# A fourth joined product in the first MLP stage, with high and low parts of the operands side by side

## What is computed

```python
def _squared_relu_mlp(h, w1, w2):
    return jnp.square(jax.nn.relu(h @ w1)) @ w2

def reference(x, norm_mix_g, norm_ffn_g, even_w_in, even_b_f, even_w_out,
              odd_w_in, odd_w_out, ffn_w_in, ffn_w_out, final_g):
    for layer in range(DEPTH):                                   # DEPTH = 2
        h = _rms_norm(x, norm_mix_g[layer])
        ...
        h = _rms_norm(x, norm_ffn_g[layer])
        x = x + _squared_relu_mlp(h, ffn_w_in[layer], ffn_w_out[layer])
    return _rms_norm(x, final_g)
```

## Time and profile before

| | |
|---|---|
| median of 3 runs | 1250.47 us (1250.42 to 1250.6) |
| the profiled execution | 1250.86 us, span of its instructions 1249.1 us |
| TensorE matmul busy | 1238.4 us, 99% |
| VectorE busy | 955.2 us, 76% |
| ScalarE busy | 768.6 us, 62% |
| GpSimd busy | 297.0 us, 24% |
| granted TensorE clock, mean | 0.998 |
| DMA moved | 238.93 MB, 191 GB/s |

### The profile page before, as it was taken

The page is one execution under the profiler, slowest core; times in us unless marked ns, Lnnn a source line. Parts: engine busy times, 40 slices in busy tenths (PEclk is TensorE's granted clock), DMA queues, the critical chain, the costliest instruction groups (busy, mean ns, idle before and its releaser), DMA issues.

```text
span 1249.1 us, 18840 instructions
## 1 busy us (share of the span) xinstructions
PE 1238.4 (99%) x7158; PEld 1080.3 (86%) x7158; DVE 955.2 (76%) x1232; ACT 768.6 (62%) x1064; POOL 297.0 (24%) x330
## 2 busy tenths in 40 slices
PE   9999999999999999999999999999999999999997
PEld 6788888898898988989898889898889889898896
DVE  6588647599779697798666797567898967869678
ACT  6688755477564575665656645456667647456474
POOL 2343653111211112101231212231221122111220
PEclk9999999999999999999999999999999999999999
DMA  7367567788988989974968588879589899898992
GB/s 246 97 137 163 136 148 191 205 210 190 225 223 219 233 189 211 225 218 114 224 135 199 131 227 180 210 155 234 101 222 243 207 203 226 217 232 202 210 215 99
DMA packets 147978, 238.93 MB, mean 191 GB/s; under 512 B 51104, under 2 KB 72872, under 8 KB 147888
## 3 DMA queue, kind: packets, MB, share of 16 engines
q0 software_dynamic: 32352, 102.79, 43.8%
q1 hardware_dynamic: 115232, 134.60, 34.1%
q10 hardware_dynamic: 304, 0.33, 0.1%
HBM read 127.57 MB, written 2.11 MB: 104 GB/s over the span
## 4 chain that ended last, share of the span: by engine, by line
PE 91%; DVE 3%; DMA 2%; issue 1%; ACT 1%; POOL 0%; SPq 0%; POOLq 0%; DVEq 0%; ACTq 0%
PE banks L1042 21%; PE banks L1420 12%; PE banks L1010 11%; PE banks L1211 7%; PE banks L969 6%; PE banks L1488 6%; PE banks L1002 5%; PE banks L1370 5%; PE banks L1151 4%; PE banks L1005 2%; PE banks L1434 2%; PE banks L1312 2%; PE banks L1178 2%; PE banks L1384 1%; DMA raw_tiles<-raw_tiles 1%
## 5 line engine op out<-in xcount | busy, mean ns | idle before, releaser
L2294 DVE TENSOR_TENSOR w<-raw_tiles,w 128x1024 fp32r<-128x1024 f32 x312 | 371.1, 1220 | 55.7 <-ACT w L1630 55.4
L1630 ACT ACTIVATE w<-raw_tiles 128x1024 fp32r<-128x1024 f32 x312 | 315.2, 1051 | 123.7 <-PE banks L1042 61.9
L1042 PE MATMUL banks<-w,arena_q 128*128 128x512 f32 x1332 | 304.3, 390 | 0.0
L3283 POOL DMA_DIRECT2D raw_tiles<-raw_tiles x176 | 152.3, 907 | 629.1 <-DVE w L2294 378.6
L1042 PEld LDWEIGHTS banks<-w,arena_q 128*128 128x128 f32 x1332 | 249.3, 188 | 51.7 <-DVE x L2620 0.4
L1420 PE MATMUL banks<-w,h_ops 128*128 128x512 f32 x672 | 154.2, 390 | 0.0
L1420 PEld LDWEIGHTS banks<-w,h_ops 128*128 128x128 f32 x672 | 125.6, 188 | 25.7
L1010 PE MATMUL banks<-h_ops,w 128*128 128x256 f32 x1152 | 140.1, 283 | 0.0
L1010 PEld LDWEIGHTS banks<-h_ops,w 128*128 128x128 f32 x1152 | 139.4, 192 | 0.7
L1002 PE MATMUL banks<-h_ops,w 128*128 128x512 f32 x288 | 102.3, 400 | 0.1
L969 PE MATMUL banks<-h_ops,w 128*128 128x256 f32 x672 | 82.0, 284 | 0.0
(11 more groups left out here) (247 smaller groups left out, 1864.9 us busy)
## 6 DMA issues: line engine op xcount, KB each, us to landing
raw_tiles<-raw_tiles POOLq DMA_DIRECT2D x176, 512.0 KB, 5.6
raw_tiles<-in_ffn_w_in SPq DMA_DIRECT2D x64, 512.0 KB, 6.3
raw_tiles<-in_ffn_w_out SPq DMA_DIRECT2D x64, 512.0 KB, 6.4
raw_tiles<-in_odd_w_in SPq DMA_DIRECT2D x32, 512.0 KB, 5.5
raw_tiles<-in_even_w_in SPq DMA_DIRECT2D x48, 256.0 KB, 3.4
raw_tiles<-in_odd_w_in SPq DMA_DIRECT2D x32, 256.0 KB, 5.0
raw_tiles<-in_odd_w_out SPq DMA_DIRECT2D x16, 512.0 KB, 6.3
raw_tiles<-raw_tiles POOLq DMA_DIRECT2D x20, 256.0 KB, 4.1
```

Source lines behind the costliest of these rows:

```text
L1042: mm = pe.matmul(bank[first + t][:, :], a_ring[a_slot(g, i)][:, a, k, P * t:P * t + P], w_slots[use_slot(use)][:, b, k, :], start=(starts ...
L1630: nc.scalar.activation(w_flat(use_slot(use), 0, half), raws[tile][:, 1024 * half:1024 * half + 1024], ACT.Copy).then_inc(m_hi, 1)
L2294: nc.vector.tensor_tensor(w_flat(use_slot(use), 1, half), raws[use_tile(key)][:, 1024 * half:1024 * half + 1024], w_flat(use_slot(use), 0, ...
L3283: pool.dma_start(raws[dst][:, part], raws[src][:, part], accum_op=ALU.add).then_inc(t_made[value][half], 16)
```

## The change

The operands' buffer becomes [block, k, 512 columns] with the low part's 256 columns directly behind the high part's, so that a joined matmul reads one run of 512. Product 7 of the first stage of wide groups becomes joined too. Its high-by-low half is in the upper half of the banks, so that ScalarE now copies (two `last_copy`), VectorE adds (two `wide_last`), and ScalarE makes one relu over the whole block in place of two from the bank. ScalarE makes both copies between the two weight halves. On VectorE the weight halves of the second stage's operand 2 move ahead of the sum S2, around the two adds. Groups 0 and 4 keep their order.

```diff
-WIDE = (1, 2, 3)
+WIDE = (1, 2, 3, 6)
...
-        h_ops = nc.alloc_sbuf_tensor_at("h_ops", [P, 8, 2, 4, 256], F32R, offset=h_at)
+        h_wide = nc.alloc_sbuf_tensor_at("h_wide", [P, 8, 4, 512], F32R, offset=h_at)
+        h_ops = h_wide[:, :, :, :].rearrange("p e k (a n) -> p e a k n", a=2)
...
-                                pe.matmul(dst.rearrange("p (q n) -> p q n", q=2), w_slots[use_slot(use)][:, 0, k, c:c + P],
-                                          h_ops[:, H_BLOCK[op], :, k, :],
+                                pe.matmul(dst, w_slots[use_slot(use)][:, 0, k, c:c + P], h_wide[:, H_BLOCK[op], k, :],
                                           start=(i < 3 and k == 0), stop=(k == 3), skip_group_check=True)
...
             def relu_last(g, b):
 
                 act.wait_ge(p_done, use_done(first_use(g, 6), b))
-                if g % CHUNKS == 0:
-                    act.wait_ge(hs_lo, 8 * (g // CHUNKS) + 4)
-                src = wide_part(6, b, LOW) if g % CHUNKS else pair_of(FIRST_X, b)
-                nc.scalar.activation(hidden_part(0, b, HIGH), src, ACT.Relu).then_inc(last_relu, 1)
+                act.wait_ge(hs_lo, 8 * (g // CHUNKS) + 4)
+                nc.scalar.activation(hidden_part(0, b, HIGH), pair_of(FIRST_X, b), ACT.Relu).then_inc(last_relu, 1)
+
+            def last_copy(g, b):
+
+                act.wait_ge(p_done, use_done(first_use(g, 6), b))
+                act.wait_ge(a_lo, 7 * g)
+                nc.scalar.activation(hidden_part(0, b, HIGH), wide_part(6, b, LOW), ACT.Copy).then_inc(last_copied, 1)
+
+            def wide_relu_last(g):
+
+                act.wait_ge(last_sum, wide_count(g) + 2)
+                block = a_blocks(1)["12"]
+                nc.scalar.activation(block, block, ACT.Relu).then_inc(last_relu, 2)
...
-                w_hi(stage + 1, 1, 0)
-                relu_last(g, 0)
-                w_hi(stage + 1, 1, 1)
-                relu_last(g, 1)
+                if g % CHUNKS:
+                    w_hi(stage + 1, 1, 0)
+                    last_copy(g, 0)
+                    last_copy(g, 1)
+                    w_hi(stage + 1, 1, 1)
+                    wide_relu_last(g)
+                else:
+                    w_hi(stage + 1, 1, 0)
+                    relu_last(g, 0)
+                    w_hi(stage + 1, 1, 1)
+                    relu_last(g, 1)
                 square(g, 3)
                 operand_hi(g, 2)
...
+            def wide_last(g, b):
+
+                v = hidden_part(0, b, HIGH)
+                dve.wait_ge(last_copied, wide_count(g) + b + 1)
+                nc.vector.tensor_tensor(v, v, wide_part(6, b, HIGH), ALU.add).then_inc(last_sum, 1)
...
                 operand_lo(g, 1)
-                hidden_operand_sum(g, S2)
-                w_lo_both(stage + 1, 1)
+                if g % CHUNKS:
+                    w_lo(stage + 1, 1, 0)
+                    wide_last(g, 0)
+                    wide_last(g, 1)
+                    w_lo(stage + 1, 1, 1)
+                    hidden_operand_sum(g, S2)
+                else:
+                    hidden_operand_sum(g, S2)
+                    w_lo_both(stage + 1, 1)
```

More of the change, by code:

```diff
@@ L687, in trunk @@
         cross_added = [sem(f"cross_added{n}") for n in range(2)]
+        last_copied = sem("last_copied")
+        last_sum = sem("last_sum")
         m_square = sem("m_square")
```

## The result

| | before | after |
|---|---|---|
| median | 1250.45 us (6 runs, 1250.21 to 1250.72) | 1260.12 us (6 runs, 1259.40 to 1261.18) |
| ratio | | 1.0076, 95% interval 1.0066 to 1.0087 |
| profiled execution, span | 1249.1 us | 1258.6 us |

The change costs 9.7 us. Forecast were 8.05 us and 1258.5 us, with a range of 1255.3 to 1261.3.

What follows compares the result with a forecast made beforehand. TensorE's instruction stream was taken as the bound, with no clock term. Delays of 5.92 (groups 1, 2, 5, 6), 1.60 and 1.2 us make 8.7, less 0.65 for layout 8.05: 1258.5 us from median 1250.47, range 1255.3 to 1261.3.

Steps and rivals of the forecast that it cites:

- The lag: Wide groups' second stage: VectorE's third operand low part 2.0 us later, from 1.2 us added work and about 1.1 us wait.
- Where it lands: Second stage on TensorE: late adds to x delay product 4 by 0.46, product 6 by 1.11, product 7 by 1.48 us.
- The end of the stage: Each wide group's second stage ends 1.48 us later; groups 1, 2, 5 and 6 together 5.92 us.
- 0.1 of restart a group: Upper end of the range: 0.1 us extra per group for restarting, beside 0.2 more lag.
- the 0.15 us from the earlier trace: Effective time from the end of a VectorE add to a waiting matmul's start, read at product 4: 0.15 us.
- Tails: Ends of groups 3 and 7: group 3 loses 1.60 us at the next norm's transposes, group 7 1.2 us.
- the end of the kernel hangs on VectorE, whose last add now waits 0.58 us: Group 7: the last add's 0.58 us wait for TensorE is subtracted from a 1.8 us delay, leaving 1.2 us.
- The layout: First-stage joined pairs: one-run reads gain 0 to 1.3 us in all; half, 0.65 us, was taken.
- The row that spoke for 0: Product 4 of g = 3: two-run pairs already take 0.348 us each, so part of the loss isn't in the addresses.
- The join: First-stage product 7: saves 0.5 to 1.3 us of TensorE time in all, but at most 0.05 us a group counts.
- the third rival: Next group's loads, such as L877, also become late, costing up to 0.5 us more a group: 1261.5 us, chance 0.06.

Runs made afterwards that it cites:

- adds alone: The kernel before with two more VectorE adds of 128x512 in each wide group, whose results nobody needs: 1254.04 us, ratio 1.0026.
- gap filled: The changed kernel with the first high and low halves of the third operand's weights made during the waits for the new chain: 1253.38 us, ratio 1.0023.
- the join alone: The changed kernel with product 7 joined but its high-by-low sum left out, ScalarE and VectorE as before: 1251.07 us, ratio 1.0004.
- Layout alone: The kernel before with the low parts directly behind the high parts and nothing else: 1250.90 us, ratio 1.0001.
- the former order on VectorE: The changed kernel with S2 and both weight halves ahead of the two adds of product 7 on VectorE: 1276.02 us, ratio 1.0204.

## Why the prediction was right

**The lag: right.** Worked out were a wait of 1.1 us and a lag of 2.0; the rows have 1.17 and 2.17 (6.80 - 4.63). Relu, square, high part and low part stand as in the sum, within 0.1 us, counted from the second operand's low part. Of the 2.17, 0.09 is not VectorE's lateness but the earlier start of the stage (it now starts 0.19 us behind the second operand's low part, and before 0.28). Lags of 1.0 (adds alone, gap filled), 2.2 and 4.6 us go with 0.42, 0.46, 1.6 and 4.5 us per group: it is the lag that sets the time, whatever makes it. Up to 2.2 us it does so through the adds to x, as forecast; at 4.6 through a weight half and the clock, as shown above.

**Where it lands: right in place and size.** Product 4 starts at 16.86 us of the stage instead of 16.35, product 6 at 28.40 instead of 27.23, product 7 at 34.13 instead of 32.67: late by 0.51, 1.17 and 1.46, where 0.46, 1.11 and 1.48 stood. One late start was not in the sum: product 3 comes at 11.22 instead of 10.91 us, as the low half of its weights (L2313 behind the low part L2633) is late. It costs nothing further, since product 4 would be later by its own add.

**The end of the stage: right, though it looks 0.12 us too small.** The stage ends 1.60 us late, not 1.48. But 0.10 us of that is what the shorter product 7 of the first stage saved: the join alone, too, lengthens the second stage by 0.09. Against the old clock group 2 loses 1.50, groups 5 and 6 0.05 more. The slow matmul behind a wait (below) is no further term, although I had put "0.1 of restart a group" in the upper bound: the 0.15 us from the earlier trace rows contain the 0.07 by which such a matmul lasted longer there.

**Tails: group 3 right, group 7 wrong.** Group 3 lost 1.76 us, 1.66 without the join's 0.10, where 1.60 stood. Group 7 lost 1.73, so 1.63 where 1.2 stood. The step that failed is "the end of the kernel hangs on VectorE, whose last add now waits 0.58 us": VectorE's lateness does reach the end, but not through that add. Here are VectorE's last two adds, what follows the first of them, and the ScalarE instruction that takes up the result of the last, before (its add is in the earlier trace rows) and after:

```profile
1240.89 0.42 DVE L2231 TENSOR_TENSOR x<-banks,x 128x256 f32<-128x256 f32 x1
1241.23 0.15 DVE L2243 SCALAR_TENSOR_TENSOR var<-ssum 128x1 f32<-128x1 f32 x1
...
1242.73 0.40 ACT L1575 ACTIVATE h_f<-x 128x256 f32<-128x256 f32 x1
```

```profile
1250.45 0.42 DVE L2250 TENSOR_TENSOR x<-banks,x 128x256 f32<-128x256 f32 x1
1250.79 0.15 DVE L2262 SCALAR_TENSOR_TENSOR var<-ssum 128x1 f32<-128x1 f32 x1
1251.10 0.42 DVE L2250 TENSOR_TENSOR x<-banks,x 128x256 f32<-128x256 f32 x1 [0.17 <-PE banks L1052]
...
1252.29 0.40 ACT L1577 ACTIVATE h_f<-x 128x256 f32<-128x256 f32 x1
```

The way to the end goes from the add before the last (1240.89, now 1250.45) through the variance, GpSimd's reciprocal root and ScalarE's scaling. From the stage's start (1203.50, now 1211.33) that variance is at 37.73 us and now at 39.46, 1.73 later, and so is the end. The last add is only 1.32 us later, and its wait shrinks from 0.58 to 0.17; but ScalarE, busy with the scaling, takes up its result 0.36 us after it is done, and now 0.77. So no part of the wait could be subtracted.

**The layout: wrong by the 0.65 us that I had taken as half of the open range.** Layout alone shows 0 of the 1.3 us. The row that spoke for 0, the two-run pair that already ran without loss in group 3, was the better guide. The rule of the Trainium skill (Advanced Engine Details and Errata, PSUM Cachelines) that any non-contiguous pattern slows matmuls significantly stands there under PSUM, the accumulation memory, while this operand is read from SBUF (`alloc_sbuf_tensor_at`): I applied it to the wrong memory, and no run here tests it. The rule of the Trainium skill for SBUF (the same page, SBUF Cachelines) gave 0, and the trace agrees with 5.66 us against 5.65.

**The join: right.** 0.10 us a group on product 7, given back in the second stage. All wide first stages together gained 0.17 us instead of 6 x 0.10, since in groups 2 and 6 product 4 waited longer, 0.2 and 0.5 us (before, 0.3 in group 5). ScalarE had waited there for a weight sum made by DMA:

```profile
414.90 1.06 ACT L1632 ACTIVATE w<-raw_tiles 128x1024 fp32r<-128x1024 f32 x1 [3.40 <-DMA raw_tiles<-raw_tiles]
...
420.31 0.60 ACT L1680 ACTIVATE arena<-banks 128x512 f32<-128x512 f32 x1 [0.46 <-PE banks L1007]
```

That is a late transfer, but not the one of the third rival, which spoke of the loads L877. It isn't made by the change as far as the traces go: the kernel before has such a wait in group 5 (ScalarE idle for 3.61 us) and the layout-only kernel in groups 3 and 5 (3.75 and 3.97).

The sum with what the runs showed: 8.7 with no layout gain, + 0.2 in groups 1, 2, 5 and 6, + 0.1 in group 3, + 0.4 in group 7, + 0.4 for the longer waits in first stages, - 0.3 in group 4 = 9.5 us. So the mechanism was right and carries 8.7 of the 9.55 us between the spans; what made 8.05 too small were above all the layout's half (0.65) and the last group's 0.4. The last two terms were in no forecast, and that they nearly cancel is luck.

## What to carry to other kernels

When TensorE never waits, ask of each product or sum moved off it what the receiving engine's queue looks like at that place, and follow the lag instruction by instruction to the next point at which TensorE waits for that engine; work and the unfilled wait of a chain count alike, and here they were about equal parts of the lag. A wait can be filled with work that is due soon anyway, which gave back 6.7 of 9.7 us. Where the lag grows, look at the weights that stand in the same queue and not only at the results: at 4.6 us they were the first to be late. And a shorter stream gains nothing where the next stage starts behind a chain that does not contain the shortened part.

## What the runs showed of the hardware

**A restart behind a wait costs 0.11 us beyond the wait.** Two matmuls of 512 columns take 0.61 us from the start of the first to the end of the second; behind a wait 0.73 (TensorE, the changed kernel):

```profile
470.69 0.61 PE L1044 MATMUL banks<-w,arena_q 128*128 128x512 f32 x2
...
471.67 0.73 PE L1044 MATMUL banks<-w,arena_q 128*128 128x512 f32 x2 [0.36 <-DVE x L2645]
```

The first of the two lasts 0.50 us and the second starts 0.34 behind it, where 0.227 is the rule. The granted clock stayed at 1.00, so it isn't the clock. What causes it the trace doesn't show.

**Where TensorE stood still for 2.5 us, its clock fell.** In the run with the former order on VectorE the granted clock was 1.00 up to product 3, then, behind 2.50 us without a matmul, 0.51 between 459.40 and 462.90, and 1.00 again; the first matmuls there follow each other in 0.427 us instead of 0.227, and product 3 took 1.7 us more than its 5.44, the 0.11 of the restart included. It came in each of the six wide groups. The waits in the changed kernel's second stages, 0.8 us at the most, left it at 1.00.

**Changing between 256 and 512 columns costs a little.** Matmuls of one width follow each other in 0.120 and 0.227 us; alternating pairs need 0.354 instead of 0.347, in fours 0.351, with the read in one run or in two. That some products run at 0.347 in spite of it remains unexplained.
